# Rotary products on all 128 rows, and the squares of the keys halved by GpSimd before VectorE sums them

## What is computed

```python
def mla_keys(c, w_uk, kn_g):
    return rms_norm(jnp.einsum('blc,chd->blhd', c, w_uk), kn_g)

def mla_scores(q_nope, q_rope, k_nope, kr):
    s = (jnp.einsum('bqhd,bkhd->bhqk', q_nope, k_nope)
         + jnp.einsum('bqhr,bkr->bhqk', q_rope, kr))
    return s * (MLA_QK ** -0.5)
```

## Time and profile before

| what | value |
|---|---|
| time, median of 3 runs | 1424.87 us (1416.44 to 1425.42) |
| the profiled execution: its time, its span | 1423.75 us, 1421.9 us |
| PE busy, share of the span | 1380.5 us, 97% |
| DVE busy | 894.3 us, 63% |
| ACT busy | 593.4 us, 42% |
| POOL busy | 206.9 us, 15% |
| mean granted TensorE clock | 0.975 |

### The profile page before, as it was taken

One profiled execution on the slowest core, in us unless ns is written; L12 is line 12 of the kernel. 1 busy time (PEld: TensorE's weight loads), 2 busy tenths in 40 slices (PEclk: granted clock), 3 DMA queues, 4 the chain that ended last, 5 costly groups with the idle time before them and its releaser, 6 DMA issues.

```text
span 1421.9 us, 23304 instructions
## 1 busy us (share of the span) xinstructions
PE 1380.5 (97%) x8148; PEld 1132.4 (80%) x8148; DVE 894.3 (63%) x1848; ACT 593.4 (42%) x1601; POOL 206.9 (15%) x330
## 2 busy tenths in 40 slices
PE   8999899999998999999999988999999999999999
PEld 6676767777776899999976666677778669999999
DVE  1346558888425787886423556588882258878964
ACT  2147657767315233330012476577762253333200
POOL 1001022111011122230000101212200121222200
PEclk9999879999989999999999998999998999999999
DMA  7330525444035343434443305344431343434342
GB/s 273 111 116 15 201 94 134 120 115 108 6 128 178 124 135 132 149 122 142 143 144 122 105 0 211 113 129 119 121 80 45 116 171 134 138 131 148 127 141 87
DMA packets 79718, 175.23 MB, mean 123 GB/s; under 512 B 11794, under 2 KB 46131, under 8 KB 78707
## 3 DMA queue, kind: packets, MB, share of 16 engines
q1 hardware_dynamic: 75952, 164.11, 35.8%
q0 software_dynamic: 3360, 9.18, 2.1%
q10 hardware_dynamic: 290, 0.45, 0.1%
HBM read 167.42 MB, written 6.29 MB: 122 GB/s over the span
## 4 chain that ended last, share of the span: by engine, by line
PE 64%; DVE 24%; ACT 9%; issue 3%; DMA 1%; SPq 0%; DVEq 0%
PE pair L515 13%; PE pair L873 9%; PE pair L874 8%; DVE area L1673 8%; PE pair L1147 7%; PE pair L988 5%; ACT area L1869 4%; PE bank L1147 3%; PE bank L909 2%; DVE area L1691 2%; PE pair L880 2%; DVE area L1697 2%; ACT area L1875 2%; PE pair L965 2%; DVE area L1689 2%
## 5 line engine op out<-in xcount | busy, mean ns | idle before, releaser
L515 PE MATMUL pair<-xg,slot 128*128 128x320 f32 x768 | 212.2, 433 | 2.6 <-DMA slot<-in_weights 1.9
L1542 DVE TENSOR_REDUCE small<-sq 128x8 f32<-128x512 f32 x256 | 168.0, 681 | 47.0 <-ACT sq L2109 45.7
L515 PEld LDWEIGHTS pair<-xg,slot 128*128 128x128 f32 x768 | 144.8, 190 | 65.4 <-issue 2.9
L2109 ACT ACTIVATE sq<-pair 128x512 f32<-128x512 f32 x256 | 152.2, 595 | 5.8 <-DVE small L1542 5.8
L1673 DVE TENSOR_TENSOR area<-slot 128x512 f32<-128x512 f32 (+1 forms) x128 | 85.4, 668 | 42.3 <-PE pair L1147 42.3
L1116 PE MATMUL pair<-sq,area 128*128 128x160 f32 x736 | 112.0, 301 | 0.0
L873 PE MATMUL pair<-wkq,area 128*128 128x288 f32 x320 | 107.6, 418 | 0.0
L1116 PEld LDWEIGHTS pair<-sq,area 128*128 128x128 f32 x736 | 102.8, 190 | 1.6 <-DVE area L1673 1.0
L874 PE MATMUL pair<-wkq,area 128*128 128x288 f32 x320 | 103.8, 406 | 0.0
L1869 ACT ACTIVATE area<-area 128x336 f32<-128x336 f32 (+6 forms) x110 | 59.2, 542 | 105.6 <-DVE area L1691 79.8
L2314 POOL DMA_INDIRECT krT<-in_cache_r,kr_rows x64 | 61.7, 965 | 223.3 <-PE pair L880 220.9
(11 more groups left out here) (457 smaller groups left out, 2707.4 us busy)
## 6 DMA issues: line engine op xcount, KB each, us to landing
slot<-in_weights SPq DMA_DIRECT2D x216, 512.0 KB, 3.5
area<-in_cache SPq DMA_DIRECT2D x160, 130.0 KB, 2.1
kept<-in_cache SPq DMA_DIRECT2D x96, 130.0 KB, 2.2
slot<-in_weights SPq DMA_DIRECT2D x18, 384.0 KB, 3.7
xg<-in_ssd_t SPq DMA_DIRECT2D x2, 1024.0 KB, 5.4
area<-in_ssd_n SPq DMA_DIRECT2D x2, 1024.0 KB, 12.8
hs_out<-area POOLq DMA_DIRECT2D x2, 1024.0 KB, 4.2
x<-in_x SPq DMA_DIRECT2D x4, 320.0 KB, 6.0
```

The source lines that it names most:

```text
L515: last = mm(out[:, 0:T], w[:, k, :], xg[:, k, :], start=(k == 0), stop=(k == KD - 1))
L1542: dve.tensor_reduce(ssk[:, t % 2, 8 * j:8 * j + 8], ksq[k % 3], AX.X, ALU.add).then_inc(V.fire(on["k_summed"]), 1)
L2109: f(ksq[k % 3].rearrange("p (a h) d -> p a h d", a=2), b4[:, :, :, NQ - at:NQ - at + 64], ACT.Square).then_inc(A.fire(on["key_free"]), 1)
```

## The change

- PE: both rotary products now use all 128 rows of `krT` and `qrep`. The rows that were left out are zero in `qrep`.
- POOL: a new function `key_fold` adds columns 32 to 63 of each head's squares to columns 0 to 31, in place, for each of the 128 pages of a layer. It waits for the square (`key_free`) and for POOL's own last instruction.
- DVE: `key_sum` waits for that (`k_folded`) and sums 32 columns a head, 256 in all.
- POOL's loop is rewritten: in each turn four folds, then the gather of the group four ahead, then, every fourth turn, the copy of the next sample's queries.

```diff
-               "key_rs": GROUPS * NB + 1, "key_full": PAGES * NB, "key_free": PAGES * NB, ...
+               "key_rs": GROUPS * NB + 1, "key_full": PAGES * NB, "k_folded": PAGES * NB, "key_free": PAGES * NB, ...
@@ tensor engine, cache_group
                         for half in range(2):
-                            rows = slice(64 * half, 64 * half + 64)
-                            last = mm(pair[:, 512 * half + 288:512 * half + 416], krT[n % KR_GROUPS][rows, :],
-                                      qrep[rows, 2 * half:2 * half + 2, :, NQ * s:NQ * s + NQ]
+                            last = mm(pair[:, 512 * half + 288:512 * half + 416], krT[n % KR_GROUPS][:, :],
+                                      qrep[:, 2 * half:2 * half + 2, :, NQ * s:NQ * s + NQ]
                                       .rearrange("p j h q -> p (j h) q"), **F)
@@ vector engine, key_sum
-                dve.wait_ge(*on["key_free"].at(l, k + 1))
-                dve.tensor_reduce(ssk[:, t % 2, 8 * j:8 * j + 8], ksq[k % 3], AX.X,
+                dve.wait_ge(*on["k_folded"].at(l, k + 1))
+                dve.tensor_reduce(ssk[:, t % 2, 8 * j:8 * j + 8], ksq[k % 3][:, :, 0:32], AX.X,
                                   ALU.add).then_inc(V.fire(on["k_summed"]), 1)
@@ gpsimd
+            def key_fold(l, k):
+
+                pool.wait_ge(*on["key_free"].at(l, k + 1))
+                pool.wait_ge(*G.last)
+                v = ksq[k % 3]
+                TTO(v[:, :, 0:32], v[:, :, 0:32], v[:, :, 32:64], ALU.add).then_inc(G.fire(on["k_folded"]), 1)
@@ gpsimd, mixers
-                for t in range(KR_GROUPS, NB * GROUPS):
-                    rope_keys(l, t)
-                    if t % 4 == 3 and 2 <= t // 4 + 1 < NB:
-                        query_slot(l, t // 4 + 1)
+                for t in range(NB * GROUPS):
+                    for j in range(4):
+                        key_fold(l, 4 * t + j)
+                    if t + KR_GROUPS < NB * GROUPS:
+                        rope_keys(l, t + KR_GROUPS)
+                    if t % 4 == 3 and t // 4 + 2 < NB:
+                        query_slot(l, t // 4 + 2)
```

More of the change, by code:

```diff
@@ L443, in trunk @@
                "o_sq": 1, "o_rs": 1, "mix_gla": 1, "score_pad": 1, "k_summed": PAGES * NB + 1,
-               "key_rs": GROUPS * NB + 1, "key_full": PAGES * NB, "key_free": PAGES * NB, "q_slot": NB, "scored": GROUPS * NB, "s_max": NB, "s_diag": NB, "s_exp": NB, "c_pad": 1,
+               "key_rs": GROUPS * NB + 1, "key_full": PAGES * NB, "k_folded": PAGES * NB, "key_free": PAGES * NB, "q_slot": NB, "scored": GROUPS * NB, "s_max": NB, "s_diag": NB, "s_exp": NB, "c_pad": 1,
                "new_ready": 1, "mk_rs": 1, "mk_ready": 1, "mq_sq": 2, "mq_rs": 2, "qm_ready": 2,
```

## The result

The changed kernel takes 1450.64 us (median of 4 runs, 1445.63 to 1459.25), the kernel before beside it 1421.91 (1416.44 to 1425.42). The ratio is 1.0248, 95% interval 1.0199 to 1.0297: the change makes the kernel slower, by 2.5%. The forecast was 1430 us and no change; the time lies inside the range, at its upper end, in the part that the range owed to rival A.

The account below looks back on a forecast made before the run. PE was taken to set the pace of the cache stage. Per layer +0.8 us for samples, +0.7 start and +1.4 end gave +2.9, +5.8 in two, on 1423.75: 1430 us predicted, range 1415 to 1452.

Parts of the forecast that it names:

- rival A: Cache stage: POOL becomes the bound, its instructions and DVE's additions delaying each other; 1441 to 1460 us, chance 0.35.
- The rotary products: PE: the pair on 128 rows takes 0.44 us instead of 0.62, saving 0.18 us a group.
- the two gaps go, since neighbours are then of one shape: PE's rotary pair: assumed that gaps of 0.09 us ahead and 0.11 us behind it vanish.
- rival C: PE: the rotary products don't get cheaper, groups stay at 4.50 us; 1434 us, chance 0.08.
- The fold: POOL: adding 256 columns takes 0.73 us a page, between ends of 0.60 and 0.87.
- POOL's wait for itself: Between folds: 0.09 us, making 0.82 with the fold; more than 0.09 would show the prediction wrong.
- POOL's group: Four folds with waits and a gather: 4.53 us, or 4.83 in a sample's fourth group.
- if each group lasts as long as the slower of the two: PE and POOL by group: a sample takes 20.85 us, the whole PE gain taken back.
- the carry: Three buffers let POOL's lag be made up in the next group, at most 2 to 3 pages.
- The sum: One layer's terms: +0.8 us for samples, +0.7 start, +1.4 end; +2.9 a layer, +5.8 in two.
- Start and end: Each layer's cache stage: POOL free late costs +0.7 us, the later last sum +1.4 us.
- its own case: The forecast without rivals: 1430 us, within 1420 to 1440, chance 0.50.

Follow-up runs that it names:

- e9: The changed kernel with a fold that adds one column of each head instead of 32, the rest left out; 1410.7 us, ratio 0.9945.
- e1: The kernel before with only the rotary products of the changed kernel, on all 128 rows; 1422.8 us, ratio 1.0007.
- e4: The changed kernel with four buffers of squares instead of three; 1426.0 us, ratio 1.0028.
- e6: The changed kernel with DVE's two additions on the scores and one copy replaced by one-input reductions of the same number of elements; 1429.5 us, ratio 1.0094.
- e5: The changed kernel with two dummy products on PE ahead of its wait at the spread of the maxima; 1446.2 us, ratio 1.02.
- e3: The changed kernel with DVE summing all 512 columns and POOL's folds written to columns nobody reads, ACT waiting for both; 1424.5 us, ratio 1.0024.

## Why the prediction was wrong, point by point

- **What bounds the kernel.** PE sets the pace before: right, and a faster sum is indeed worth nothing (e9).
- **The rotary products.** The pair costs 0.44 us as predicted (315.62 to 316.06 in the changed kernel), without a gap ahead of it. The step "the two gaps go, since neighbours are then of one shape" fails in two groups of four, whose neighbours have 64 rows or columns, and one of the other two runs into ACT's exponentials: 0.72 us a sample were to be saved, and e1 shows 0.06 lost. For the sample this is rival C (no gain), with another cause: between 128-row neighbours the products did get cheaper.
- **The fold.** 0.73 forecast, 0.726 measured. POOL's wait for itself is 0.14, not 0.09, which the prediction had named as a sign of being wrong: folds in a row start 0.87 apart.
- **POOL's group.** 4.53 forecast; four times 0.87 and 0.96 are 4.44, and 0.14 for the gather's wait makes 4.58. The size is right, by luck in part: the dearer waits (0.20 a group) are made up by the gather, 1.10 with its wait instead of 1.25. POOL is busy 15.8 us a sample, about 18.6 with those waits. Yet the sample is 22.45 to 24.13 and not 20.85.
- **The step that failed** is "if each group lasts as long as the slower of the two", with 0.10 us a sample against the carry. An engine in series does not only add work that must fit; it makes the way from square to sum longer, 1.29 us (0.73 + 0.14 + 0.42) instead of 0.68, in a ring of three buffers that already stood at its limit at the maximum: ACT waited for a sum 7 times in the layer before the change, so once in nearly every one of its 8 samples, right behind the maximum. That row was read as small, where it showed that the ring had no slack at that place. Of the changed sample's 22.45 us, 1.46 are idle PE at the spread of the maxima; the 20.99 that are left are e1's 20.91, without any fold, but for 0.08. So POOL does not stretch each group, and the whole price lies at one place. The sum had set 0.72 us a sample for POOL's slower groups against 0.72 gained by the rotary products; neither came, and that these two errors cancel is luck. The term was 0.10 us a sample; it measures 1.60 with the clock at 1.00, and e4, e6 and e9 each take most or all of it away by more buffers, an earlier maximum, or a shorter fold.
- **Start and end** were put at +0.7 and +1.4 us a layer. From the first product with a page to the first maximum it is +3.2 and +3.1 us in the two layers, with the first, longest wait of PE in it (2.49 us for a maximum); from the last L874 to the next stage's first product it is 24.73 us before and after, so the end costs nothing.
- **The clock** had no term at all. It costs 1.69 us in each sample in which it falls, and e5 gives back 10.5 us in both layers.
- **Rival A** was the right side and about the right size (1441 to 1460), with the contention turned round. It let POOL's instructions wait for DVE's additions, as in the earlier trace rows; in the changed kernel no fold lasted over 0.75 us (in e3 and e4 13 of 256 did, up to 1.00). DVE's additions and copies waited for the folds (an addition lasted up to 1.38 us), and the price came through the maximum (e6: 21.4 of 37.1 us) and not through POOL's group. Nor was POOL the bound, as e3 shows with the same work at 21.44.
The Trainium skill, "SBUF — State Buffer", Who interferes with whom, says that a reduction never contends with GpSimd, and that a two-input addition and some copies do. The runs agree: 0.42 us for each reduction (e6), up to 1.38 for the addition, 0.60 to 1.18 instead of 0.19 for the copy.

The savings of the runs don't add up, since buffers and port take away the same idle 1.46 us, and with it most falls of the clock: buffers 21.4, port 21.4, clock 10.5, of 37.1. That the measured time lies inside the range is no sign for the forecast's mechanism: its own case was given 1420 to 1440.

## What to carry to other kernels

Before an engine is put between two others, add up the way round the ring of buffers at its tightest place (here the one long DVE instruction of a sample), not only the work of each engine; a short wait that comes back once per period, as ACT's did here, can be the sign that the ring has no slack there. Look at what the added engine runs beside: additions and copies ahead of a long instruction may wait for it. Here an idle PE of 1.5 us often cost that much again in the granted clock.

## What was not expected of the hardware

- With the same idle stretch of 1.46 us on PE the granted clock fell to 0.50 for some 3 us in some samples (24.13 us) and stayed at 1.00 in others (22.45). Idle stretches of 0.50 us once a sample (e4, e6) left it at 1.00; the one fall that each of these two kernels has in a layer comes behind a longer stretch in the first sample (1.76 to 2.56 us). In e5 stretches of 2.23 and 2.35 us there led to no fall, so the length of the stretch does not decide it alone.
The Trainium skill, "TensorE: Matmul & The Clock Gate", A second HAM failure mode: psum-queue depth-cycling, tells of a kernel in which short idle times of PE between groups let the clock swing between its two levels. The trace agrees, and e5 shows that dummy products in the idle time stop it.
- POOL's fold of 8 columns a partition takes 0.216 us and that of 256 takes 0.726, which is 2.06 ns a column between them.
- A float32 product pair of 128*128 costs 0.44 us between 128-row neighbours; beside 64-row and 64-column neighbours it costs more: 0.54 us from L879 to L898 and 0.53 to L908 in e1, and 0.36 instead of 0.26 from L898 to L916.
